# Moving the third product's copy, the modulation rows and the pooling residual in a two-block fp32 transformer kernel

## The reference, cut to what matters

```python
def modulated_sublayer(x, mod, g_pre, g_post, fn, weight):
    shift, scale, gate = mod[:, 0], mod[:, 1], mod[:, 2]
    h = rmsnorm(x, g_pre) * (1.0 + scale) + shift
    y = rmsnorm(fn(h), g_post)
    return x + weight * (1.0 + gate) * y

for i in range(2):
    mod = (silu(c) @ ada_w[i] + ada_b[i]).reshape(B, 9, 1024)
    x = modulated_sublayer(x, mod[:, 0:3], ..., lambda h: swiglu(h, w_in[i, 0], w_out[i, 0]), 0.5)
    x = modulated_sublayer(x, mod[:, 3:6], ..., pool_mixer if i == 0 else mla_mixer, 1.0)
    x = modulated_sublayer(x, mod[:, 6:9], ..., lambda h: swiglu(h, w_in[i, 1], w_out[i, 1]), 0.5)
```

## Time and profile before

| what | value |
|---|---|
| median of 3 runs | 2932.2 us (2930.58 to 2932.82) |
| the profiled execution | 2932.32 us |
| its span | 2930.5 us |
| TensorE busy | 2805.9 us, 96% |
| VectorE busy | 2185.0 us, 75% |
| ScalarE busy | 1448.7 us, 49% |
| GpSimd busy | 401.0 us, 14% |
| mean granted TensorE clock | 0.984 |
| memory traffic | 123 GB/s over the span |

### The profile page before, as it was taken

One profiled execution on the slowest core, in us unless ns is written; L12 is line 12 of the kernel. 1 busy time (PEld: TensorE's weight loads), 2 busy tenths in 40 slices (PEclk: granted clock), 3 DMA queues, 4 the chain that ended last, 5 costly groups with the idle time before them and its releaser, 6 DMA issues. The chain is left out here.

```text
span 2930.5 us, 42964 instructions
## 1 busy us (share of the span) xinstructions
PE 2805.9 (96%) x16774; PEld 2451.4 (84%) x16774; DVE 2185.0 (75%) x3427; ACT 1448.7 (49%) x2390; POOL 401.0 (14%) x297
## 2 busy tenths in 40 slices
PE   8999989999999999799999999999899999999999
PEld 7998778998889988677799988787788778877887
DVE  7888778888778877899687755387677663866773
ACT  6555235555255542566465632464555435555552
POOL 0010111000101001100300000404300233141003
PEclk9999999999999999999999999999999999999999
DMA  7675733665636656200245432402211232022113
GB/s 271 194 224 172 238 126 76 207 203 174 233 115 214 208 168 215 73 12 19 101 119 162 145 107 87 136 15 83 91 52 58 96 127 72 30 94 72 54 56 115
DMA packets 103065, 367.40 MB, mean 125 GB/s; under 512 B 11984, under 2 KB 14800, under 8 KB 102352
## 3 DMA queue, kind: packets, MB, share of 16 engines
q1 hardware_dynamic: 73968, 262.95, 25.8%
q0 software_dynamic: 26304, 90.19, 11.7%
q10 hardware_dynamic: 2592, 11.51, 1.1%
HBM read 354.12 MB, written 6.29 MB: 123 GB/s over the span
## 5 line engine op out<-in xcount | busy, mean ns | idle before, releaser
L464 ACT ACTIVATE w_hi<-raw 128x1024 fp32r<-128x1024 f32 x351 | 366.8, 1053 | 320.1 <-DMA raw<-stream_in 179.1
L485 POOL TENSOR_TENSOR w_lo<-raw,w_hi 128x1024 fp32r<-128x1024 f32 x109 | 274.2, 2522 | 1265.1 <-ACT w_hi L464 1265.0
L506 PE MATMUL psum<-h_hi,w_hi 128*128 128x256 f32 (+1 forms) x1609 | 352.3, 329 | 8.5 <-DVE h_lo L699 3.4
L506 PE MATMUL psum<-h_lo,w_hi 128*128 128x256 f32 (+1 forms) x1609 | 345.4, 325 | 0.0
L506 PE MATMUL psum<-h_hi,w_lo 128*128 128x256 f32 (+1 forms) x1609 | 345.2, 325 | 0.0
L479 DVE TENSOR_TENSOR w_lo<-raw,w_hi 128x1024 fp32r<-128x1024 f32 x202 | 247.2, 1227 | 83.1 <-ACT w_hi L464 82.9
L506 PE MATMUL psum<-t_hi,w_hi 128*128 128x256 f32 (+1 forms) x1536 | 284.9, 300 | 19.9 <-ACT sq L1156 7.5
L464 ACT ACTIVATE w_hi<-xr 128x1024 fp32r<-128x1024 f32 x202 | 213.5, 1057 | 160.6 <-DVE xr L1271 68.6
L506 PEld LDWEIGHTS psum<-h_hi,w_hi 128*128 128x128 f32 x1609 | 251.0, 188 | 44.1 <-DVE w_lo L479 5.8
L506 PE MATMUL psum<-t_hi,w_lo 128*128 128x256 f32 (+1 forms) x1536 | 283.3, 299 | 0.0
L506 PEld LDWEIGHTS psum<-h_lo,w_hi 128*128 128x128 f32 x1609 | 252.0, 188 | 26.9
(11 more groups left out here) (527 smaller groups left out, 5568.4 us busy)
## 6 DMA issues: line engine op xcount, KB each, us to landing
raw<-stream_in SPq DMA_DIRECT2D x351, 512.0 KB, 3.4
ada_raw<-ada_in POOLq DMA_DIRECT2D x128, 512.0 KB, 5.3
xr<-stream_in SPq DMA_DIRECT2D x122, 512.0 KB, 4.6
xr<-stream_in POOLq DMA_DIRECT2D x40, 512.0 KB, 5.5
ada_in_t<-ada_in SPq DMA_DIRECT2D x8, 512.0 KB, 12.0
x_held<-X ACTq DMA_DIRECT2D x2, 2048.0 KB, 6.8
X<-x_held ACTq DMA_DIRECT2D x2, 2048.0 KB, 7.9
X<-xT_in SPq DMA_DIRECT2D x4, 512.0 KB, 5.5
```

Source lines behind the costliest of these rows:

```text
L464: act.activation(w_hi[:, u % RING], tile, ACT.Copy, scale=-1.0 if u in negated else 1.0).then_inc(hi_ready, 1)
L485: pool.tensor_tensor(w_lo[:, u % RING], source[u][0], w_hi[:, u % RING].bitcast(F32), ALU.subtract).then_inc(lo_ready, 1)
L506: mm = pe.matmul(dst, w[wi], m[mi], start=(first and n == 0), stop=(last and n == total - 1), skip_group_check=skip)
```

## The change

1. In pair 0 of each feed-forward stage ScalarE copies the third product (u2) right after p5, ahead of `split_hi(u + 5)` and of the high half of T4. In the other pairs it stays where it is.
2. The rows in pairs become a table, `PAIR_ROWS`. In ffn0 the pairs 3 to 8 get a third row (`ada_pair_dve(dve, L, j, 2)`, behind `sum_2_dve`), 22 rows in place of 16, and the down projection has 26 in place of 32. ffn1 and ffn2 keep 16 and 24. In all three stages unit 1 of the down projection has no row any more, and the others are spread anew. GpSimd issues a pair's pieces by the same table, ahead of the accumulating load of the next pair.
3. In the residual between ffn0 and the pooling mixer GpSimd adds the product to X; VectorE multiplies, scales and makes the low half, in a new order.

```diff
@@ post_dve @@
+            if after == "pool":
+                pool_residual_dve(dve, L, y, after, columns, shift)
+                return
...
+        def pool_residual_dve(dve, L, y, after, columns, shift):
+
+            def move(c):
+                if c >= 2:
+                    dve.wait_ge(x_ready.sem, x_ready.at((L, c - 2)))
+                dve.tensor_tensor(ta[:, c % 2], y(c), psum[:, 6], ALU.mult).then_inc(residual_moved, 1)
+            move(0)
+            move(1)
+            dve.wait_ge(spread.sem, spread.at(((L, "post"), "s")))
+            for c in range(NC):
+                dve.wait_ge(x_ready.sem, x_ready.at((L, c)))
+                scale_dve(dve, after, c, columns)
+                if c + 2 < NC:
+                    move(c + 2)
+                if c:
+                    low_dve(dve, after, c - 1, shift)
+            low_dve(dve, after, NC - 1, shift)
+
+        def pool_residual_gpsimd(pool, L):
+
+            for c in range(NC):
+                pool.wait_ge(residual_moved, c + 1)
+                x_ready.give(pool.tensor_tensor(X[:, c], X[:, c], ta[:, c % 2], ALU.add), (L, c))
...
-        FIRST_PAIR = {"ffn0": 1, "ffn1": 1, "ffn2": 1}
+        PAIR_ROWS = {"ffn0": (0, 2, 2, 3, 3, 3, 3, 3, 3, 0), "ffn1": (0,) + 8 * (2,) + (0,),
+                     "ffn2": (0,) + 8 * (2,) + (0,)}
...
-        DOWN_ROWS = {"ffn0": (0, 1, 1, 2, 2, 1, 2, 2, 1, 2, 2, 1, 2, 2, 1, 2, 2, 1, 2, 2, 1, 0, 0, 0),
-                     "ffn1": (0, 1, 1, 1, 1, 1, 1, 2, 1, 1, 2, 1, 1, 2, 1, 1, 1, 2, 1, 1, 1, 0, 0, 0)}
+        DOWN_ROWS = {"ffn0": (0, 0, 1, 2, 1, 1, 2, 1, 1, 2, 1, 1, 2, 1, 1, 2, 1, 1, 2, 2, 1, 0, 0, 0),
+                     "ffn1": (0, 0, 1, 1, 2, 1, 1, 2, 1, 1, 2, 1, 1, 2, 1, 1, 2, 1, 1, 1, 1, 0, 0, 0)}
...
@@ pair_act @@
             keep_act(act, L, j, "p5", 1, "v2")
+            if j == 0:
+                keep_act(act, L, j, "u2", 2, "g2")
             split_hi(act, u + 5)
...
             if j == 0:
                 combine_hi_act(act, L, T4)
-            keep_act(act, L, j, "u2", 2, "g2")
+            else:
+                keep_act(act, L, j, "u2", 2, "g2")
...
@@ pair_dve @@
             sum_2_dve(dve, L, j + 1)
+            ada_pair_dve(dve, L, j, 2)
             up_sum_dve(dve, L, j)
...
@@ ffn_pool @@
             for j in range(PAIRS):
-                if ADA[L] and FIRST_PAIR[L] <= j < PAIRS - 1:
+                for _ in range(PAIR_ROWS[L][j] if ADA[L] else 0):
                     ada_piece(pool, t)
-                    ada_piece(pool, t + 1)
-                    t += 2
+                    t += 1
                 add_weights(pool, L, j + 1)
...
@@ gpsimd @@
             ffn_pool(pool, "ffn0")
+            pool_residual_gpsimd(pool, "ffn0")
             add_squares_gpsimd(pool, "pool")
```

More of the change, by code:

```diff
@@ L292, in kernel_program @@
         parts_negated, odd_added = sem("parts_negated"), sem("odd_added")
+        residual_moved = sem("residual_moved")
         t2_copied = sem("t2_copied")
@@ L1020, in ada_pair_dve @@
         def ada_pair_dve(dve, L, j, m):
-            if ADA[L] and FIRST_PAIR[L] <= j < PAIRS - 1:
-                ada_blocks_dve(dve, L, FIRST_ROWS[L] + 2 * (j - FIRST_PAIR[L]) + m, 1)
+            if ADA[L] and m < PAIR_ROWS[L][j]:
+                ada_blocks_dve(dve, L, FIRST_ROWS[L] + sum(PAIR_ROWS[L][:j]) + m, 1)
         def ada_down_dve(dve, L, k):
             if ADA[L]:
-                ada_blocks_dve(dve, L, FIRST_ROWS[L] + 2 * (PAIRS - 1 - FIRST_PAIR[L]) + sum(DOWN_ROWS[L][:k]), DOWN_ROWS[L][k])
+                ada_blocks_dve(dve, L, FIRST_ROWS[L] + sum(PAIR_ROWS[L]) + sum(DOWN_ROWS[L][:k]), DOWN_ROWS[L][k])
         def pair_banks(j):
```

## The result

The changed kernel takes 2941.4 us (median of seven; 2938.8 to 2943.6) against 2932.2 for the kernel before: ratio 1.0034 [1.0022, 1.0046], slower by 0.34%. The profiled execution took 2939.1 us, its span is 2937.3 against 2930.5. The forecast was 2935.5 with a range of 2924 to 2947, so the range holds the time and the sign is that of the forecast's sum. The forecast was 6 us too low, and that small difference hides two errors that partly cancel: the pairs of ffn0 cost 10 us more than forecast, the rest gained some 4 us more. That the time falls inside the range is in part luck.

The account below looks back on a forecast made before the run. VectorE's chain, not TensorE, was taken to set the end of ffn0. Gains in the other parts against +21.8 us for the pairs summed to +3.1 us on 2932.3, forecast 2935.5 us, range 2924 to 2947.

Parts of the forecast that it names:

- What bounds ffn0: First pair to second down-projection unit of ffn0: VectorE's chain, without slack, sets the end, not TensorE.
- Part 4: Pairs 3 to 8 of ffn0: third rows +6.8, later accumulating load +15.8, absorbed waits -0.8, together +21.8 us.
- rival C: ffn0's pairs: accumulating load behind a 512 KB piece lands at 7.4 us, VectorE stands 4.1 not 2.6; 2944.5 us; 21%.
- Its counterargument: ffn0's pairs: the stretch in which the accumulating load now falls is the pair's quiet one.
- Part 1: Pair 0, third product's copy moved ahead: -3.6 us in ffn3, -1.2 in ffn0 to ffn2, +1.5 for the clock.
- The 1.5 us for the clock: ffn1 and ffn2: longer a_lo(7) waits of 2 to 3 us may lower the clock, +1.5 us (bounds 0 and 3.4).
- Part 2: Unit 1 of the down projections without a row: TensorE's 1.49 us wait falls to 0.35, three stages, -3.4 us.
- Part 3: ffn0's down projection with 26 instead of 32 rows: w_lo waits gone, -5.6 us; VectorE's last chunk in time, -1.4.
- The prediction's own mark: ffn0's down projection: 116 us from a_lo(7) to its end instead of 124, without w_lo waits.
- The -1.4 for VectorE's last chunk: End of ffn0's down projection: VectorE no longer behind TensorE's column sums, -1.4 us (bound 0).
- Part 5: Residual ahead of the pooling mixer: GpSimd's add cuts the period from 2.65 to 2.0 us, -4.0; clock -1.0.
- The sum: All terms: -3.6 - 1.2 + 1.5 - 3.4 - 5.6 - 1.4 + 21.8 - 4.0 - 1.0 = +3.1 us.

Follow-up runs that it names:

- e5: Kernel before, with GpSimd's accumulating load in pairs 3 to 8 of ffn0 held until the sum for product 2 is made; 2959.6 us, ratio 1.0092.
- e7: Kernel before, with the second piece of pairs 3 to 8 of ffn0 and the accumulating load held until the next pair's product 2 sum; 2964.7 us, ratio 1.0111.
- e12: Kernel before, with ffn0's accumulating load of pairs 4 to 9 held until the fourth low half of its own pair, clear of SyncE's load; 2969.2 us, ratio 1.0128.
- e1: Changed kernel with two rows again in each of pairs 1 to 8 of ffn0 and 32 in its down projection; 2919.2 us, ratio to kernel before 0.9953.
- e3: Kernel before with only the third product's copy moved in pair 0; 2927.9 us, ratio 0.9983.
- e9: Kernel before with only unit 1's row of the down projections moved elsewhere in ffn0, ffn1 and ffn2; 2931.8 us, ratio 1.0000.
- e6: Changed kernel with its row tables alone, the third product's copy and the residual as before; 2952.5 us, ratio to kernel before 1.0070.
- e8: Changed kernel, accumulating load ahead of the third piece, third row only in pairs 4, 6, 8 of ffn0, 29 down-projection rows; 2918.6 us, ratio to kernel before 0.9948.

## Why the prediction was right, and where it was not

- **What bounds ffn0.** Right: VectorE had no slack in the pairs, every delay there came out at a_lo(7) and stayed. e5, e7 and e12 add no work at all to any engine and lose 27 to 38 us by their ratios; in their traces unit 2 comes 27.2, 29.2 and 32.4 us later.
- **Part 4, the term that was mis-sized.** The forecast was +21.8 for rows and load. Measured by e1 and the changed kernel it is +33.1 (301.16 less 268.02). The rows, with the small waits beside them, cost 8.6 for 6.8 - 0.8. The step that failed is "It lands 5.1 to 7.4 us after its issue, median 5.5 [...] I take 5.9": the median is over forty loads, the six in question already had 6.2 before, the load had been moved behind SyncE's and behind a piece, and it landed after 7.2 to 8.0. The VectorE waits are 24.5 us and not 15.8. The landing is rival C's, 7.4 us, and its waits of 4.1 are those measured. Its counterargument, that the stretch is the quiet one of the pair, was what misled: SyncE's load into the tile of a11 is released by the same sum behind which the third row, its piece and the accumulating load now come, 1.9 us later, so they meet in every pair. That such a meeting can stretch the load is shown by e5 against e12, with VectorE's standing still in e12 as the reservation; how much of the 7.4 us it makes in the changed kernel, beside the piece, stays open.
- **Part 1.** Forecast -3.6 - 1.2 + 1.5 = -3.3; measured alone -5.0 [-7.6, -2.3] (0.9983). In ffn3 the delay against before shrinks from 12.2 us at pair 0 to 8.5 at unit 2, by 3.7, as forecast. The 1.5 us for the clock were not paid: in the traces of e3 and of the changed kernel waits of 1.34 and 1.36 us at a_lo(7) left it at 1.00. These waits were forecast as 2 to 3 us; another 0.7 stood ahead of them, at a copy of ScalarE's (e3's ffn1, changed kernel's ffn1 and ffn2). From the column sums of one stage to unit 2 of the next, ffn1 and ffn2 give 1.6 and 2.2 us in e3's trace, for some 1.0 forecast for both together, while its ffn0 down projection came out 2.9 us longer, with the clock at the lower level twice.
- **Part 2.** Forecast -3.4; the waits of 1.49 us became 0.34 in three stages, as forecast, but e9 allows at most 2.6. In ffn0 more than half was lost again in the down projection, where the clock fell behind a wait for w_lo.
- **Part 3.** Forecast -5.6 up to the column sums; measured -6.9 (110.0 for 116.9 us), no w_lo wait left; the waits alone were 5.6. The prediction's own mark, 116 us from a_lo(7) to the end, is met: 411.12 less 295.08. The -1.4 for VectorE's last chunk shows as -1.2: that is what e6, with the chunk in time and the residual of before, saves behind the column sums. In e1, with the residual of the change but the chunk 1.4 us late, the step took 28.6 us instead of 24.8, since behind a wait of 0.98 us in the column sums the clock also stood at 0.50 for some 6 us.
- **Part 5.** Forecast -5.0 with the clock's share; measured alone -5.6 [-8.5, -2.3], and -4.4 in the traces (24.8 us in the changed kernel for 29.15 in e6). The period is 2.11 us for 2.0 forecast. h_lo was not slowed. The Trainium skill (GPSIMD Engine Reference, Specifications) has GpSimd share its SBUF interfaces with VectorE and contend with VectorE instructions that have two SBUF inputs. The trace agrees that the two meet (1.73 for 1.26 us), but the one that takes longer here is GpSimd.
- **The sum.** +3.1 against a measured +10.0 [6.5, 13.5] by the ratio; part 4 was 11.3 too small, the others together some 4 too small in gain. The second block's span came out 1.7 shorter, which no edit explains and which is within what two profiles differ by.

## What to carry to other kernels

When work is added ahead of a DMA in an in-order queue, count what every instruction in that queue now waits for: here one load that followed a piece it had nothing to do with cost 24.5 us, and swapping the two turned 0.3% slower into 0.6% faster. And take the landing time of a moved load from the place that it moves to: ask which other load the same event releases and what stands ahead of it in its own queue, for a median over the whole kernel knows nothing of either. A wait that is taken away in front of a saturated engine is not yet a gain; follow the same engine to its next one.

## What the runs showed of the hardware

- A load of GpSimd's queue that was issued 0.27 us behind one of SyncE's moved nothing for 2 us, while SyncE's moved 100 packets; such loads landed after 8.1 us (e5, median of six) instead of 5.3 (e12). The Trainium skill (DMA: Bandwidth & Descriptors, Queues, rings and completion order) says that a DMA engine takes turns between its queues, packet by packet. These traces don't settle whether it was so here: most of the 2 us is no contest between queues, for in e12, with no other packet in flight, the accumulating load moved none in its first 1.5 us either, as q0 is absent from that window and all of it stands in the 4 us behind (view of the DMA queues, 142.80 to 146.80):

```profile
q0 software_dynamic: 144, 0.52, 81.6%
```

- A GpSimd add of two SBUF tiles took 1.73 us beside VectorE instead of 1.26, while VectorE's scalar_tensor_tensor with two SBUF tiles kept its 0.74. In rows 12 it was VectorE's tensor_tensor that rose from 0.69 to 1.72. The GpSimd add that it met there is the next one after that of rows 12:

```profile
434.06 1.27 POOL L815 TENSOR_TENSOR std<-std,sq 128x512 f32<-128x512 f32 x1 [0.48 <-ACT sq L737]
```

  In both places the instruction that started later is the one that took longer: VectorE's at 434.16 behind GpSimd's at 434.06 before, GpSimd's at 424.12 and 426.24 behind `h_lo` at 423.96 and 426.07 in the changed kernel. No run puts this to the test by turning the order round.
- Waits of TensorE of 1.34 and 1.36 us were not followed by a lower granted clock; those of 1.88 us in the kernel before were in two stages of four (rows 6 shows the two; in ffn0 and ffn2 it stayed at 1.00). The length of the wait alone does not decide it: behind one of 2.25 us in the kernel before and one of 2.26 us in e8, both for w_lo and both at the end of ffn0's down projection, the granted clock was 1.00 and 0.50:

```profile
377.00:380.00 3.00, 3.00 (x13) 2.50 (x14) 2.90 (x6) 1.02 (x3) 0.53 (x1) 1.00 0.89 303
375.60:378.60 3.00, 3.00 (x9) 2.35 (x8) 2.90 (x7) 1.78 (x3) 0.53 (x1) 0.50 0.97 378
```
